# A transformer pair on one core: units and silu of the last block in another order

## The chip, the cores and the metric

The kernel runs on one core of a Trainium2 chip. The metric is the device time of one execution in microseconds (us). Below, PE is TensorE's matmul, DVE is VectorE, ACT is ScalarE, POOL is GpSimd and SP issues the loads of the weights.

## What is computed

Two blocks over 512 tokens of width 1024, in float32. The first is a mixer of banded attention and pooling with a convolutional feed-forward layer. The second, which matters here, adds to x the result of a mixer with four heads in two branches:

```python
hn = rms_norm_2(x, w_norm)
proj = jnp.einsum("bsd,de->bse", hn, w_in.astype(f32))
q_a, k_a, v_a, z_a, b_a, a_a, q_b, k_b, v_b, z_b = jnp.split(proj, idx, axis=-1)
qkv = jax.nn.silu(causal_depthwise_conv(jnp.concatenate([q_a, k_a, v_a], -1), conv_w))
beta = jnp.transpose(jax.nn.sigmoid(b_a), (0, 2, 1))
g = -jnp.exp(a_log) * jax.nn.softplus(a_a + dt_bias)
o_a = gated_delta_rule_chunked(q_a, k_a, v_a, g, beta)
o_a = rms_norm_2(o_a, gdn_norm_w) * jax.nn.silu(z_a)
o_b = diff_attention(q_b, k_b, v_b, lam)          # q_b, k_b normed and rotated
o_b = rms_norm_2(o_b, subln_w, SUBLN_EPS) * (1.0 - lam_init)
o_b = o_b * jax.nn.silu(z_b)
return jnp.einsum("bse,ed->bsd", jnp.concatenate([o_a, o_b], -1), w_out)
```

## The kernel before

Activations lie transposed, features on the 128 partitions and the 512 tokens along the free axis. Every product with weights is made in **units** of 128 x 1024 weights: eight steps (one for each tile of 128 input features), each of three matmuls of 512 columns, because weights and activations are split in a high and a low part (Wh and Wl, Hh and Hl; L514, L515, L517). SP loads a unit into `raw`, one of four buffers; ACT rounds it to Wh (L1697, `round_unit`); DVE takes the rest as Wl (L1029, `split`). Both do that two units ahead of the unit that PE works on. Behind its unit, DVE reads the sum out of its bank times the norm's factors (L1068).

The last block starts at about 703 us. DVE and ACT make the norm's tiles Hl and Hh; PE multiplies the first two units (c0 and c1 of the first head) along with them (`units_together`, L549), and adds up the squares (L568). The factors are a power on GpSimd (L2097), turned into a row by PE (`norm_row`, L585) and copied to RB by DVE (L1063). Without RB no unit can be read.

Then `second_block` runs four **stages**, one for each head a. Stage a has the prep of head a (decays, key products, the inverse of a triangular matrix in six levels) and, from the second stage on, the scan and the differential attention of head b = a - 1. A head has eight units: c0, c1, c2 (convolution inputs of q, k, v), z0 and z1 (gates of the two branches), Kr, Qb, v (second branch). Stage a computes c2 (first head only), z0, z1, Kr, Qb and v of head a, and c0, c1, c2 of the next head.

The order of the instructions is written out by `Rounds`: in each round every chain (prep, pair norms, scan, diff) goes one piece further, and then as many unit steps are issued as the pace says (PACE_PREP, PACE_SCORES). Each engine's program is made by the same rounds, so in a round PE, DVE and ACT have their parts of the same chains and of the same units. Engines are in order: a piece that waits holds up all that stands behind it. A unit's read and the rounding and splitting two units ahead are unit steps and fall where the count puts them.

The names that the prediction uses:
- `gate_chain`: PE multiplies the gates' rows (24 matmuls, L733 to L735), DVE copies them (L1323), PE turns them (into bank 5), DVE and ACT make beta and the logarithms `glog` (L1352), PE sums them (L751), DVE copies `gcum` (L1357).
- prep: the row of gcum (L759) into bank b6, DT (L1366), `sums` of squares (L826), kk (L769), LT (L1392) and its strips (L1394, L1395, ACT L1926), masks up to LmT (L1408); per level y (PE L778, ACT copy L1933) and t (PE L797, DVE L1422 and L1425, called T); level five has t at L801 and L804; kt and qk behind level two, then Kb (L1450), Kd, AT.
- pair norms: `pair sums` (PE L878), DVE L1471, a power on GpSimd (L2175), DVE L1476. The weighted copy of Kr and Qb and its square are ACT L2032 and L2033.
- scan of head b: for each of four tiles a product (L893), VN on DVE (L1485), products with Kd and QG (L898, L900), state St (L1492).
- diff of head b: maxima (L1544), exponentials (ACT L2000), Wd (L1563), turned (L952), product (L959). `out_norm` scales Oa or Od (L1509), PE turns it (L764), and DVE multiplies with Zs (L1514).
- `silu_gates(i)`: ACT makes Zs = silu(Zr) of head i once z0 and z1 are read (L1889). It is the first piece of the prep of stage i + 1, and for the last head it stands ahead of the tail.
- the convolution: ACT takes the first tap of C (L2023), DVE three more (L1579); c2's read first takes what is left of c1's taps.

In the tail the scan and diff of the last head run beside the output projection (L999, L1000, L1002), whose activations Hh are made from O by ACT (L2054).

Of the kernel before, what the change touches and what calls it, by code (L numbers as in the profile page):

```python
# [18 lines left out]
P = 128  # L19
# [7 lines left out]
GH = 4  # L27
# [54 lines left out]
PACE_SCALARS, PACE_END = 3, 1.5  # L82
PACE_SCORES, PACE_PREP = (None, 1.9, 1.9, 1.25), (1.5, 1.7, 1.7, 0.8)
# [66 lines left out]
def program(nc, ctx, x_in, w_units, w_ba, cols_in, mats_in, rope_in, rows_in, relb_in, counts_in,  # L150
# [144 lines left out]
    bank_of.update({G_UP + j: UP_BANKS[j % 6] for j in range(N_UP)})  # L295

# [4 lines left out]
    def sum_read(g):  # L301

        return bank_read[g % 2], g // 2 + 1
# [158 lines left out]

    UNIT_PLACE = {n: j for j, n in enumerate(("c0", "c1", "c2", "z0", "z1", "Kr", "Qb", "v"))}

# [17 lines left out]
    def second_block(rounds_of, first, chains_of, unit_of):  # L482

        for a, b in STAGES:
            st = rounds_of(a, b)
            st.scanning = st.scoring = b is not None
            st.dense = [unit_of(st, a, n) for n in ("c2", "z0", "z1", "Kr", "Qb", "v")[a > 0:]]
            if a + 1 < GH:
                st.dense += [unit_of(st, a + 1, n) for n in ("c0", "c1", "c2")]
# [13 lines left out]
    def tensor_program():  # L503
# [38 lines left out]
        def units_together(n0, g0, lags, turn, squares=None):  # L542


            banks = [group_begins(g0 + u) for u in range(len(lags))]

# [3 lines left out]
            for m in range(KT + max(lags)):  # L550
                now = [(u, m - lag) for u, lag in enumerate(lags) if 0 <= m - lag < KT]
                if m < KT:
                    pe.wait_ge(*norm_hh.at(turn, m))
                for u, k in now:
                    weights_ready(n0 + u, k)
                    product(u, k, Wh, Hh, start=k == 0, stop=False)
                    product(u, k, Wl, Hh, start=False, stop=False)
                if m < KT:
                    pe.wait_ge(*norm_dv.at(turn, ("hl", m)))
                for u, k in now:  # L560
# [168 lines left out]
        def gate_chain(st):  # L729
            pe.wait_ge(*lam_dv.at(0, "ba_lo"))  # L730
            for k in range(KT):
                w = slice(2 * GH * k, 2 * GH * (k + 1))
                pe.matmul(PS[0:2 * GH, 4, :], ba_h[:, w], Hh[:, k, :], start=k == 0, stop=False)  # L733
                pe.matmul(PS[0:2 * GH, 4, :], ba_h[:, w], Hl[:, k, :], start=False, stop=False)
                ins = pe.matmul(PS[0:2 * GH, 4, :], ba_l[:, w], Hh[:, k, :], start=False,  # L735
                                stop=k == KT - 1)
            ins.then_inc(*gate_pe.tick(0, "rows"))
            yield
            yield
# [174 lines left out]
        def diff(st, i):  # L914
# [11 lines left out]
            pe.wait_ge(*sum_read(G_P2 + 8 * i + UNIT_PLACE["v"]))  # L926
# [44 lines left out]
        def unit_of(st, a, name):  # L971
            j = UNIT_PLACE[name]
            n, g = U_P2 + 8 * a + j, G_P2 + 8 * a + j
# [3 lines left out]
        norm_row(2)  # L977
# [42 lines left out]
    def vector_program():  # L1020
# [564 lines left out]
        def read_of(st, a, name):  # L1585
            g = G_P2 + 8 * a + UNIT_PLACE[name]
# [28 lines left out]
        def unit_of(st, a, name):  # L1615
            n = U_P2 + 8 * a + UNIT_PLACE[name]
# [71 lines left out]
    def scalar_program():  # L1688
# [193 lines left out]
        def silu_gates(i):  # L1882

            ac.wait_ge(*sum_read(G_P2 + 8 * i + UNIT_PLACE["z0"]))
            ac.wait_ge(*sum_read(G_P2 + 8 * i + UNIT_PLACE["z1"]))
# [5 lines left out]
        def prep(st, i):  # L1891
# [20 lines left out]
            if i:  # L1912
                silu_gates(i - 1)
# [100 lines left out]
        def read_of(st, a, name):  # L2014
            g = G_P2 + 8 * a + UNIT_PLACE[name]
# [20 lines left out]
        def unit_of(st, a, name):  # L2036
            n = U_P2 + 8 * a + UNIT_PLACE[name]
# [216 lines left out]
def _layout(np, inp):  # L2254
# [16 lines left out]
    p2 = _units(np, big).reshape(8, GH, P, KT, P)[[0, 1, 2, 3, 7, 5, 4, 6]]  # L2271
    p2 = p2.transpose(1, 0, 2, 3, 4).reshape(32, P, KT, P)
# [72 lines left out]
```

## Time and profile before

| | us |
|---|---|
| median of 3 runs | 1111.91 |
| lowest and highest | 1110.41, 1115.26 |
| the profiled execution | 1109.57 |
| its span | 1108.1 |
| PE busy | 1062.4 (96%) |
| DVE busy | 646.0 (58%) |
| ACT busy | 443.2 (40%) |
| mean granted clock of PE | 0.989 |

Times of single instructions come from the one profiled execution. In a row of the timeline the bracket at the end is how long the engine sat idle before the instruction, and what ended that. In the chain of waits each piece is what the next one waited for; "issue" is time for which the profile has no record.

### The profile page before, as it was taken

The page shows a single profiled execution, that of the slowest core. Times are in us where ns is not written, and L with a number is a line of the kernel's source. Part 1 is how long each engine was busy: PE and PEld are TensorE (multiplying, and loading weights), DVE is VectorE, ACT ScalarE, POOL GpSimd, SP SyncE. Part 2 cuts the span into 40 slices and gives each one's busy share as a digit, 9 for nine tenths or more (in the row PEclk, how much of TensorE's full clock was granted, in tenths as well). Part 3 has the DMA queues.
Part 4 walks back from the last instruction along what each step waited for, and adds up shares of the span by engine and source line. Part 5 has one row for each costly group of instructions (what it writes and reads, how often), then busy time and mean ns, then how long its engine had stood idle before and what let it go on. Part 6 is the DMA issues. An engine that isn't in the chain of part 4 may idle for free.

```text
span 1108.1 us, 15316 instructions
## 1 busy us (share of the span) xinstructions
PE 1062.4 (96%) x6212; PEld 842.2 (76%) x6212; DVE 646.0 (58%) x1121; ACT 443.2 (40%) x773; POOL 89.5 (8%) x77
## 2 busy tenths in 40 slices
PE   7999999999999999999999999989989989988998
PEld 6777777778788888888888888867766866866776
DVE  6645454556437788777772122655576566466574
ACT  6233232344443544444442222443264254354531
POOL 1000000000210000000001000001120120120210
PEclk9999999999999999999999999999999989989999
DMA  8221313122321333333322233131111111110102
GB/s 333 84 83 57 95 58 95 58 77 78 112 95 57 96 114 97 113 96 95 95 95 88 103 114 114 36 95 58 58 39 54 62 39 39 59 56 21 58 20 76
DMA packets 25429, 90.72 MB, mean 82 GB/s; under 512 B 2880, under 2 KB 3136, under 8 KB 25232
## 3 DMA queue, kind: packets, MB, share of 16 engines
q1 hardware_dynamic: 23328, 83.90, 24.0%
q0 software_dynamic: 592, 3.54, 0.8%
q10 hardware_dynamic: 1440, 2.31, 0.6%
q8 instruction: 49, 0.80, 0.3%
q14 instruction: 20, 0.16, 0.0%
HBM read 87.64 MB, written 2.10 MB: 81 GB/s over the span
## 4 chain that ended last, share of the span: by engine, by line
PE 88%; DVE 7%; ACT 3%; issue 2%; POOL 0%; DMA 0%; ACTq 0%; DVEq 0%; POOLq 0%
PE PS L514 23%; PE PS L517 22%; PE PS L515 22%; PE PS L549 5%; PE PS L640 1%; DVE Wl L1029 1%; PE PS L769 1%; PE PS L1002 1%; PE PS L999 1%; PE PS L1000 1%; PE PS L653 1%; PE PS L946 1%; DVE C L1579 1%; ACT Wh L1697 1%; PE PS L663 1%
## 5 line engine op out<-in xcount | busy, mean ns | idle before, releaser
L514 PE MATMUL PS<-Hh,Wh 128*128 128x512 f32 x856 | 353.0, 412 | 0.6 <-ACT M L1817 0.6
L517 PE MATMUL PS<-Hh,Wl 128*128 128x512 f32 x856 | 336.1, 393 | 0.0
L515 PE MATMUL PS<-Hl,Wh 128*128 128x512 f32 x856 | 336.0, 392 | 0.0
L1029 DVE TENSOR_TENSOR Wl<-raw,Wh 128x1024 fp32r<-128x1024 f32 x155 | 188.9, 1224 | 193.9 <-ACT Wh L1697 192.1
L514 PEld LDWEIGHTS PS<-Hh,Wh 128*128 128x128 f32 x856 | 162.2, 189 | 44.4 <-issue 11.5
L1697 ACT ACTIVATE Wh<-raw 128x1024 fp32r<-128x1024 f32 x155 | 161.4, 1051 | 71.8 <-PE PS L517 60.9
L517 PEld LDWEIGHTS PS<-Hh,Wl 128*128 128x128 f32 x856 | 161.9, 189 | 35.2
L515 PEld LDWEIGHTS PS<-Hl,Wh 128*128 128x128 f32 x856 | 162.7, 190 | 31.6 <-issue 2.2
L514 PE MATMUL PS<-Ah,Wh 128*128 128x512 f32 x176 | 69.8, 396 | 0.0
L515 PE MATMUL PS<-Al,Wh 128*128 128x512 f32 x176 | 69.8, 396 | 0.0
L517 PE MATMUL PS<-Ah,Wl 128*128 128x512 f32 x176 | 69.8, 396 | 0.0
L1816 ACT ACTIVATE sq<-PS 128x512 f32<-128x512 f32 x16 | 9.6, 598 | 88.8 <-PE PS L517 88.8
L1068 DVE TENSOR_TENSOR tmp<-PS,RB 128x512 f32<-128x512 f32 x44 | 30.3, 692 | 21.0 <-PE PS L517 18.8
L1844 ACT ACTIVATE conv<-conv 128x512 f32<-128x512 f32 x22 | 13.9, 632 | 71.0 <-DVE conv L1271 71.0
L2107 POOL MEMSET ssum<- 128x512 f32 x2 | 1.1, 528 | 481.5 <-DVE Hl L1256 255.6
L517 PEld LDWEIGHTS PS<-Ah,Wl 128*128 128x128 f32 x176 | 33.1, 188 | 8.1
L515 PEld LDWEIGHTS PS<-Al,Wh 128*128 128x128 f32 x176 | 33.1, 188 | 8.1
L514 PEld LDWEIGHTS PS<-Ah,Wh 128*128 128x128 f32 x176 | 33.1, 188 | 8.1
L549 PE MATMUL PS<-Hh,Wh 128*128 128x512 f32 x72 | 30.1, 419 | 7.6 <-DVE Wl L1134 7.3
L1831 ACT ACTIVATE conv<-tmp,cols 128x512 f32<-128x512 f32 x44 | 35.2, 802 | 5.5 <-DVE tmp L1068 5.5
L1768 ACT ACTIVATE sq<-sq,nmax 128x512 f32<-128x512 f32 (+3 forms) x32 | 17.7, 554 | 44.3 <-DVE nmax L1194 43.7
L1271 DVE SCALAR_TENSOR_TENSOR conv<-tmp,cols,conv 128x510 f32<-128x510 f32 x44 | 33.0, 750 | 1.6
(310 smaller groups left out, 1479.0 us busy)
## 6 DMA issues: line engine op xcount, KB each, us to landing
raw<-in_w_units SPq DMA_DIRECT2D x155, 512.0 KB, 3.5
relb<-in_rel POOLq DMA_DIRECT2D x1, 2048.0 KB, 9.4
out<-X ACTq DMA_DIRECT2D x8, 256.0 KB, 2.1
X<-in_x SPq DMA_DIRECT2D x3, 512.0 KB, 7.4
X<-in_x SPq DMA_DIRECT2D x2, 256.0 KB, 4.3
raw<-in_w_units SPq DMA_DIRECT2D x2, 256.0 KB, 4.6
rope<-in_rope POOLq DMA_DIRECT2D x1, 512.0 KB, 4.0
mats<-in_mats POOLq DMA_DIRECT2D x1, 384.0 KB, 3.4
```

What stands on the lines that cost most here:

```text
L514: pe.matmul(bank, Wh[:, s, w], rhs[0](r), start=first and j == 0, stop=False)
L515: pe.matmul(bank, Wh[:, s, w], rhs[1](r), start=False, stop=False)
L517: ins = pe.matmul(bank, Wl[:, s, w], rhs[0](r), start=False, stop=last and end)
L549: return pe.matmul(banks[u], w[:, s, own], h[:, k, :], **ends)
L640: pe.matmul(PS[:, 2 + a, 0:nk], Q2[r, tok(qt)], K2[r, 0:nk], start=True, stop=True).then_inc(*att_pe.tick(i, ("scores", n, a)))
L1029: dv.tensor_tensor(Wl[:, s, :], raw[:, s, :], Wh[:, s, :].bitcast(F32), sub).then_inc(unit_split, 1)
L1068: return dv.tensor_tensor(dst, PS[:, bank_of[g], :], RB[:], mult).then_inc(bank_read[g % 2], 1)
L1271: dv.scalar_tensor_tensor(out=c[:, 2:], in0=y[:, 0:S - 2], scalar=col(C_CONV + 4 * j), in1=c[:, 2:], op0=mult, op1=add).then_inc(up_taps, 1)
L1697: ac.activation(Wh[:, s, :], raw[:, s, :], ACT.Copy).then_inc(unit_rounded, 1)
L1768: ac.activation(w, w, ACT.Exp, bias=nmax[:, b + a:b + a + 1], scale=1.0, accum_out=rsum[:, b + a:b + a + 1]).then_inc(*att_ac.tick(i, ("ex ...
L1831: ac.activation(conv[:, p % 2, j % 2, :], tmp[:, j % 2, :], ACT.Identity, bias=col(C_CONV + 4 * j + 3), scale=col(C_CONV + 4 * j + 2)).the ...
L1844: ac.activation(c, c, ACT.Gelu_apprx_tanh).then_inc(up_gelu, 1)
```

## The change

It touches the last block alone. The units are put in an order of their own by stage (`STAGE_UNITS`, `UNIT_PLACE`): z1 of a head moves to the start of the next head's stage (for the last head it is the last unit of its own), v comes ahead of Kr, z0 behind Qb. The paces change. The matmuls of the gates' rows move out of `gate_chain` in between the norm's tiles, and `norm_row` moves into `gate_chain`, behind four steps of the third unit (c2), for which that unit gets bank 6. `silu_gates` of the head before moves behind the silu of C, and that of the last head into the tail's fourth round. The weights are laid out in the new order.

```diff
+STAGE_UNITS = [[(a, x) for x in ("c2", "z0", "v", "Kr", "Qb")] if a == 0 else
+               [(a - 1, "z1"), *((a, x) for x in ("v", "Kr", "Qb", "z0", *("z1",) * (a == GH - 1)))]
+               for a in range(GH)]
+for a in range(GH - 1):
+    STAGE_UNITS[a] += [(a + 1, x) for x in ("c0", "c1", "c2")]
+UNIT_PLACE = {u: n for n, u in enumerate([(0, "c0"), (0, "c1"), *sum(STAGE_UNITS, [])])}
...
-PACE_SCALARS, PACE_END = 3, 1.5
-PACE_SCORES, PACE_PREP = (None, 1.9, 1.9, 1.25), (1.5, 1.7, 1.7, 0.8)
+PACE_GATES, PACE_END = (4, 2, 3, 3, 4, 5, 2, 1), 1.5
+PACE_SCORES, PACE_PREP = (None, 1.9, 1.9, 1.5), (1.3, 1.9, 1.9, 1.3)
...
+    bank_of[G_P2 + 2] = 6
...
-                while st.chains:
-                    st(PACE_SCALARS)
+                for pace in PACE_GATES:
+                    st(pace)
...
+                if turn == 2 and m < KT:
+                    w = slice(2 * GH * m, 2 * GH * (m + 1))
+                    pe.matmul(PS[0:2 * GH, 4, :], ba_h[:, w], Hh[:, m, :], start=m == 0, stop=False)
+                    pe.matmul(PS[0:2 * GH, 4, :], ba_l[:, w], Hh[:, m, :], start=False, stop=False)
                 if m < KT:
                     pe.wait_ge(*norm_dv.at(turn, ("hl", m)))
+                if turn == 2 and m < KT:
+                    ins = pe.matmul(PS[0:2 * GH, 4, :], ba_h[:, w], Hl[:, m, :], start=False,
+                                    stop=m == KT - 1)
...
         def gate_chain(st):
-            pe.wait_ge(*lam_dv.at(0, "ba_lo"))
-            for k in range(KT):
...
-            ins.then_inc(*gate_pe.tick(0, "rows"))
-            yield
+            yield
+            norm_row(2)
             yield
             pe.wait_ge(*gate_dv.at(0, "rows"))
...
+            else:
+                pe.wait_ge(*sum_read(G_P2 + 2))
             row_of(b6, gcum[:, i, :]).then_inc(*prep_pe.tick(i, "g"))
...
         units_together(U_P2, G_P2, LAGS_LAST, 2, up_squares)
-        norm_row(2)
...
                 ac.activation(C3[:], C3[:], ACT.Silu).then_inc(*prep_ac.tick(i, "silu"))
+                if i:
+                    silu_gates(i - 1)
                 yield
...
             if i:
-                silu_gates(i - 1)
                 yield from idle(2)
...
+        def last_gates():
+            yield from idle(3)
+            silu_gates(GH - 1)
+
         st = Rounds()
-        silu_gates(GH - 1)
-        st.chains = [split_outputs(st), scan(st, GH - 1), diff(st, GH - 1)]
+        st.chains = [split_outputs(st), scan(st, GH - 1), diff(st, GH - 1), last_gates()]
```

## Rows read from the trace of the kernel before

**Rows 1.** The page, part 1: busy us, share of the span, instructions.

```profile
PE 1062.4 (96%) x6212; PEld 842.2 (76%) x6212; DVE 646.0 (58%) x1121; ACT 443.2 (40%) x773; POOL 89.5 (8%) x77
```

**Rows 2.** Windows: length, busy time by engine, PE's clock, DMA share, GB/s.

```profile
800.00:885.00 85.00, 78.57 (x704) 61.30 (x704) 52.80 (x116) 37.09 (x79) 14.66 (x10) 0.98 0.17 52
885.00:970.00 85.00, 78.57 (x690) 61.10 (x687) 51.86 (x116) 37.08 (x79) 14.44 (x10) 0.96 0.16 50
970.00:1042.00 72.00, 63.36 (x617) 48.62 (x614) 43.55 (x106) 35.06 (x76) 13.49 (x10) 0.93 0.14 44
```

**Rows 3.** Timeline of PE: start, us, what, and idle before it with its releaser.

```profile
723.47 0.65 PE L585 MATMUL PS<-ident,rstd 128*128 128x128 f32 x4 [1.34 <-POOL rstd L2097]
743.42 0.37 PE L751 MATMUL PS<-glog,mats 128*128 128x16 f32 x2 [2.26 <-DVE glog L1352]
764.47 0.45 PE L778 MATMUL PS<-head_Ti,head_LmT 32*32 32x32 f32 x32 [1.69 <-DVE head_LmT L1408]
809.54 0.49 PE L898 MATMUL PS<-head_VN,head_Kd 128*128 128x128 f32 x2 [3.94 <-DVE head_VN L1485]
845.79 1.16 PE L769 MATMUL PS<-C 128*128 128x128 f32 x8 [2.09 <-DVE head_Ti L1425]
893.53 0.79 PE L898 MATMUL PS<-head_VN,head_Kd 128*128 128x128 f32 x2 [3.94 <-DVE head_VN L1485]
978.84 0.80 PE L898 MATMUL PS<-head_VN,head_Kd 128*128 128x128 f32 x2 [4.64 <-DVE head_VN L1485]
1013.47 0.44 PE L952 MATMUL PS<-ident,head_Wd 128*128 128x128 f32 x2 [1.31 <-DVE head_Wd L1563]
```

**Rows 4.** The chain that ended last, 884 to 895: start, us, what.

```profile
884.37 0.76 DVE C L1579
...
886.69 0.61 DVE Yc L1068
...
888.07 1.28 ACT L1889
...
889.36 1.06 ACT Zs L1889
890.42 0.95 ACT Wh L1697
...
891.43 1.10 issue
```

**Rows 5.** A window behind the third stage's start.

```profile
892.00:900.00 8.00, 6.47 (x17) 4.72 (x18) 6.38 (x11) 4.38 (x5) 4.03 (x3) 0.57 0.22 66
```

**Rows 6.** Timelines of PE and DVE at the entry, 723 to 731.

```profile
723.88 0.48 PE L733 MATMUL PS<-Hh,ba_h 128*8 128x512 f32 x1
729.51 0.39 PE L514 MATMUL PS<-Hh,Wh 128*128 128x512 f32 x1
...
724.16 0.69 DVE L1063 COPY RB<-PS 128x512 f32<-128x512 f32 x1 [1.83 <-PE PS L585]
...
730.40 0.67 DVE L1323 COPY tmp<-PS 8x512 f32<-8x512 f32 x1
```

**Rows 7.** Timelines of ACT and DVE in the first head, 758 to 765.

```profile
758.07 0.72 ACT L2032 ACTIVATE heads_Kr<-Yc,cols 128x512 f32<-128x512 f32 x1 [4.60 <-DVE Yc L1068]
...
760.29 1.23 DVE L1029 TENSOR_TENSOR Wl<-raw,Wh 128x1024 fp32r<-128x1024 f32 x1 [0.98 <-ACT Wh L1697]
761.43 0.68 DVE L1392 TENSOR_TENSOR head_LT<-PS,head_DT 128x512 f32<-128x512 f32 x1
...
763.77 0.65 DVE L1408 TENSOR_TENSOR head_LmT<-head_Ti,mats 128x512 f32<-128x512 f32 x1
```

**Rows 8.** Timelines of DVE and POOL in the first head, 773 to 779.

```profile
773.19 0.69 DVE L1450 TENSOR_TENSOR head_Lo<-PS,eg 128x512 f32<-128x512 f32 x1 [0.66 <-PE PS L764]
...
775.59 2.90 POOL L2175 TENSOR_TENSOR rqk_b<-rqk_b,half 128x16 f32<-128x16 f32 x1 [0.18 <-DVE rqk_b L1471]
```

**Rows 9.** Timeline of DVE in the second stage, at the sums.

```profile
823.02 0.17 DVE L1377 TENSOR_SCALAR rqk<-PS 128x8 f32<-128x8 f32 x1 [1.12 <-PE PS L826]
```

More of the change, by code:

```diff
@@ L460, in program @@
     N16 = GH * NT
-    UNIT_PLACE = {n: j for j, n in enumerate(("c0", "c1", "c2", "z0", "z1", "Kr", "Qb", "v"))}
     def unit_steps(st, name, unit):
@@ L486, in second_block @@
             st.scanning = st.scoring = b is not None
-            st.dense = [unit_of(st, a, n) for n in ("c2", "z0", "z1", "Kr", "Qb", "v")[a > 0:]]
-            if a + 1 < GH:
-                st.dense += [unit_of(st, a + 1, n) for n in ("c0", "c1", "c2")]
+            st.dense = [unit_of(st, *u) for u in STAGE_UNITS[a]]
             if b is None:
                 st.chains.append(first(st))
-                while st.chains:
-                    st(PACE_SCALARS)
+                for pace in PACE_GATES:
+                    st(pace)
+                assert not st.chains
             st.chains = chains_of(st, a, b)
@@ L545, in units_together @@
             banks = [group_begins(g0 + u) for u in range(len(lags))]
+            if turn == 2:
+                pe.wait_ge(*lam_dv.at(0, "ba_lo"))
             def product(u, k, w, h, **ends):
@@ L557, in units_together @@
                     product(u, k, Wl, Hh, start=False, stop=False)
+                if turn == 2 and m < KT:
+                    w = slice(2 * GH * m, 2 * GH * (m + 1))
+                    pe.matmul(PS[0:2 * GH, 4, :], ba_h[:, w], Hh[:, m, :], start=m == 0, stop=False)
+                    pe.matmul(PS[0:2 * GH, 4, :], ba_l[:, w], Hh[:, m, :], start=False, stop=False)
                 if m < KT:
                     pe.wait_ge(*norm_dv.at(turn, ("hl", m)))
+                if turn == 2 and m < KT:
+                    ins = pe.matmul(PS[0:2 * GH, 4, :], ba_h[:, w], Hl[:, m, :], start=False,
+                                    stop=m == KT - 1)
+                    if m == KT - 1:
+                        ins.then_inc(*gate_pe.tick(0, "rows"))
                 for u, k in now:
@@ L729, in gate_chain @@
         def gate_chain(st):
-            pe.wait_ge(*lam_dv.at(0, "ba_lo"))
-            for k in range(KT):
[L732 to L736, printed above, removed]
-            ins.then_inc(*gate_pe.tick(0, "rows"))
             yield
+            norm_row(2)
             yield
@@ L925, in diff @@
             pe.matmul(s1, mat(K_SWAP), Qs[:, i % 2, :], start=True, stop=True).then_inc(*diff_pe.tick(i, "qs"))
-            pe.wait_ge(*sum_read(G_P2 + 8 * i + UNIT_PLACE["v"]))
+            pe.wait_ge(*sum_read(G_P2 + UNIT_PLACE[i, "v"]))
             if i:
@@ L971, in unit_of @@
         def unit_of(st, a, name):
[L972 to L973 removed]
+            n, g = U_P2 + UNIT_PLACE[a, name], G_P2 + UNIT_PLACE[a, name]
             yield from unit_steps(st, name, unit(n, g))
         units_together(U_P2, G_P2, LAGS_LAST, 2, up_squares)
[L977 removed]
         second_block(lambda a, b: Rounds(), gate_chain, chains_of, unit_of)
@@ L1585, in read_of @@
         def read_of(st, a, name):
-            g = G_P2 + 8 * a + UNIT_PLACE[name]
+            g = G_P2 + UNIT_PLACE[a, name]
             def conv_read():
@@ L1615, in unit_of @@
         def unit_of(st, a, name):
-            n = U_P2 + 8 * a + UNIT_PLACE[name]
+            n = U_P2 + UNIT_PLACE[a, name]
             yield from unit_steps(st, name, unit(n, read_of(st, a, name)))
@@ L1882, in silu_gates @@
         def silu_gates(i):
-            ac.wait_ge(*sum_read(G_P2 + 8 * i + UNIT_PLACE["z0"]))
-            ac.wait_ge(*sum_read(G_P2 + 8 * i + UNIT_PLACE["z1"]))
+            ac.wait_ge(*sum_read(G_P2 + UNIT_PLACE[i, "z0"]))
+            ac.wait_ge(*sum_read(G_P2 + UNIT_PLACE[i, "z1"]))
             if i:
@@ L2014, in read_of @@
         def read_of(st, a, name):
-            g = G_P2 + 8 * a + UNIT_PLACE[name]
+            g = G_P2 + UNIT_PLACE[a, name]
             def first_tap_of():
@@ L2036, in unit_of @@
         def unit_of(st, a, name):
-            n = U_P2 + 8 * a + UNIT_PLACE[name]
+            n = U_P2 + UNIT_PLACE[a, name]
             yield from unit_steps(st, name, unit(n, read_of(st, a, name)))
@@ L2269, in _layout @@
     big = np.concatenate([w2[:, :n], w2[:, n + 2 * GH:]], axis=1)
-    p2 = _units(np, big).reshape(8, GH, P, KT, P)[[0, 1, 2, 3, 7, 5, 4, 6]]
-    p2 = p2.transpose(1, 0, 2, 3, 4).reshape(32, P, KT, P)
+    p2 = _units(np, big).reshape(8, GH, P, KT, P)
+    part = {n: j for j, n in enumerate(("c0", "c1", "c2", "z0", "Qb", "Kr", "v", "z1"))}
+    p2 = np.stack([p2[part[x], a] for a, x in sorted(UNIT_PLACE, key=UNIT_PLACE.get)])
     wout = _units(np, inp["w_out_2"][0])
```

## The prediction

> **What bounds the kernel now.** The page comes first. TensorE (PE) is busy 96% of the span [rows 1], so the time is PE's work plus what PE waits plus what it loses to a lower clock. Everything the diff touches lies in the last block, from about 703 us to the end, and each of those three has to be read there. The windows by head give idle and clock: PE idles 6.4 us of 85 in the second head's stage, and 8.6 of 72 in the fourth's at a mean clock of 0.93 [rows 2]. The timeline of PE, kept to instructions that waited, then names the waits [rows 3]: at the entry 1.34 us for the norm's factors and 2.26 for the gates' logarithms; 1.69 in the first head for the masks of the inverse (LmT); 3.94, 3.94 and 4.64 at the start of the three later stages, each time on VN, the scan's first vector step; and 2.09 in the middle of the second and third heads. In the fourth stage the window's idle is 8.64, of which 4.64 is the start; the other 4.0 are five waits of 0.4 to 1.3, the 1.31 among them.
>
> **What a start is made of.** The chain of waits over the third stage's start is to be read downwards [rows 4]: DVE drains three taps of C (0.76 each) and reads the unit, ACT takes the first tap, loads a table (1.28), computes Zs (1.06), and only then rounds the next unit (0.95); DVE splits it (1.10), and VN is queued behind that split. So the silu of the gates stands in the path of a vector step with which it has nothing to do.
>
> **A unit of cover.** A unit has eight steps of three matmuls. The 24 gate-row matmuls run from 723.88 to 729.51 [rows 6], 0.23 each, so a step is 0.69 us. I counted, from the rounds and paces, which steps stand between two chain instructions on PE, and what DVE and ACT have queued between theirs. The order so counted for the kernel before agrees with its timelines; for the changed one it gives the terms below.
>
> **1. Entry.** The 24 gate-row matmuls move in between the norm's tiles. PE is the slower engine there too, so they only change place: 5.6 us less behind the factors' row, 5.6 more ahead: nothing. The first four steps of the third unit go ahead of the factors' row, 2.75 us, and cover the 1.34 wait. But between that row and the turning of the gates' rows PE now has two steps left, where it had 24 matmuls and six steps. DVE's part between the two is unchanged: from the copy of RB at 724.16 to that of the rows, which ends at 731.07, and PE's row began 0.7 earlier, together 7.6 us [rows 6, 3]. PE's cover is 0.4 + 1.4. A new wait of 5.8 us. Behind it, eleven steps (third unit's rest excepted) now stand where eight did, so the 2.26 for the logarithms goes. Entry: 5.8 - 1.34 - 2.26 = +2.2. Bounds: +1.5 if the later copy is met a step sooner, +3 if the slower clock behind the wait delays the next read.
>
> **2. First head, the inverse's start.** In the new order the read of Kr stands behind LT, and the split of two units ahead behind that read, ahead of the masks. From the end of kk: LT, strips and masks 3.0 (LT starts at 761.43, LmT ends at 764.42), and in between them a read, 0.7, weighted copy and square on ACT, 1.3 (from 758.07 to a rounding's length before the split), the rounding 1.0 and the split 1.1 (760.29 to 761.43): with small hand-overs 7.0 [rows 4, 7]. PE has one step, four transposes and three steps, 3.2. With 0.2 by which DVE is late for sums: wait 4.0, for 1.69: +2.3. Bounds +1 and +3.
>
> **3. First head, the pair sums.** Qb's read now stands behind Kb, Kd and AT on DVE, and PE's pair sums three rounds further on have two steps of cover. From Kb at 773.19 DVE is taken until the pair factors start on GpSimd at 775.59, 2.2 without the hand-over [rows 8]; then read, weighted copy and square, 2.0. A new wait of 2.2; bounds 0 and 2.5.
>
> **4. First head, levels four to six.** The pair factors take GpSimd 2.90 [rows 8] and T4 is queued behind them; c0's read, its first tap and a rounding stand ahead of Y5 on ACT (0.7 + 0.7 + 1.0 for 2.5 of cover), and a split and two taps ahead of T5 on DVE. Waits of 0.4, 2.0 and 1.0: +3.4; bounds 0 and 4.
>
> **5. Starts of the later stages.** Silu's load and Zs leave the path: 2.34 [rows 4]. At the second stage two of the three taps are already taken in the prep rounds (1.5 more), so 3.94 falls to about 0.2. At the third and fourth a split now sits ahead of the last reads of the head before and hands 0.4 back: 3.94 to 2.0, and 4.64 to 2.1, since the pace of 1.5 puts one more step ahead of the wait. Together 12.5 to 4.3: -8.2. Zs goes behind C's silu, where ACT needs no second load; the rounding there waits for z1's read and Zs and comes 1.7 later. Queued behind it on DVE are the scan's second state and the first maximum; behind those DVE idled 1.12 for the sums [rows 9], which hides it but for half a microsecond that PE's own cover there takes. Without that cover it costs 1.7 a head. The mid-head waits of 2.09 have the same queues ahead of them as before: nothing.
>
> The 1.28 of the load ends where Zs starts, 888.07 to 889.36 [rows 4]. The Trainium skill, "ScalarE: Activation LUTs", section "What ACT_TABLE_LOAD costs", puts a drain of about 1.38 us behind every load. The trace doesn't show it here. By the page each start would give 1.4 more, and the time would be some 3 us less than my sum.
>
> **6. Fourth stage.** One unit more (z1 of the head before) fills it, at 1.5 steps a round for 1.25. But the splits fall elsewhere: one ahead of the fourth VN (0.8), and Kr's read, weighted copy, rounding and split now all stand ahead of the scaling of Oa (1.0 + 1.1 + 1.3 + 0.7 against three steps: 2.1); then 0.9 for Wd, 0.2, and 1.4 for Y5 behind Qb's copy. 5.5 for 4.0: +1.5. Bounds -3 and +3.
>
> **7. Clock.** Behind each of the three starts the granted clock fell from 2.4 to 1.2 GHz for a while, as 892 to 900 shows (0.57), and once behind the small waits at 1013 to 1020 [rows 2, 5]. By the three windows that is 85 x 0.02 + 85 x 0.04 + 72 x 0.07 = 10.1, of which some 0.6 fell into waits: 9.5 us. Waits of 2.26 and 2.09 drew no fall. Changed: the two waits of 4 us and more in the first head draw one each, 2.5 (between 1.7, that of 800 to 885, and 3.4, that of 885 to 970); the fourth stage keeps its 1.7; 0.7 for the levels' waits. 7.4: -2.1.
>
> **8. Tail.** The last silu goes three rounds back on ACT, behind the splitting of the outputs. No row shows it there; Zs and its load take 2.3, and ACT is the least busy of the three engines [rows 2]: nothing; bounds -0.5 and +1.
>
> **Sum.** 2.2 + 2.3 + 2.2 + 3.4 - 8.2 + 1.5 - 2.1 = +1.3 us on the profiled execution, whose span is 1108.1 and whose time is 1109.6. That is 2.3 below the median, 1111.9, from which the forecast is therefore 1113.2.
>
> **Rivals.**
> A, faster. The new waits are chains over three engines, and I let each link begin where the one before ends. If DVE and ACT reach them earlier than that, half of 4.0 + 2.2 + 3.4 + 5.5 = 15.1 goes, and one fall of the clock with it: 7.5 + 2.5 less, 1103. For it: DVE is busy 53 and ACT 37 of the 85 us of a stage [rows 2], and the starts' gain is read straight off a chain. Against: each is at most a few instructions long and queued in order. Chance 0.25.
> B, slower: the clock. The kernel before had one fall behind small waits. If the waits of 2 us (pair sums, levels, two starts) draw three falls more at 2.5, and the two long ones 3.4 instead of 2.5, it is 7.5 + 1.8 more, 1122.5; with the long ones alone it is 1115, with one short fall 1117.5, and from the second on the kernel is slower. For it: the fourth stage. Against: 2.26 and 2.09 twice without. Chance 0.2.
> C, the change doesn't do what it says: the silu still holds up the units, now by z1's read. If DVE's idle isn't there, three heads lose 1.7 each: 1118.3. Chance 0.08.
> The forecast: 0.47, with its own range of 1108 to 1118 from the bounds of terms 2, 4 and 6.
>
> **How the numbers follow.** The forecast is the likeliest, 1113.2. Leaving the far halves of A and B out, the range is 1104 to 1121. About 0.5%, 5.6 us, is what a measurement tells from no change: faster than 1106.3 are most of A and a little of the forecast, 0.26; slower than 1117.5 most of B, half of C and a little of the forecast, 0.27; between, 0.47.
>
> **What the profile after would show.** Step 1: an idle of about 5.8 before the transposes of the gates' rows into bank 5, none before those of the factors or the sums of glog. 2: about 4 before the first matmuls of the inverse. 3, 4: 2 before the pair sums, 2 before the level-five products. 5: under 2.5 before each first Kd product, and half as many table loads per later head. 6: 2 before the turning of Oa in the last stage. 7: granted clock under 1 behind steps 1 and 2 and none from 890 to 900. The prediction is wrong if 5.8 isn't there, or if first-head idle sums to less than 8.

## The result, and the profile after

The changed kernel takes 1117.84 us (median of 4 runs, 1117.39 to 1119.57) for 1111.41 beside it (4 runs): ratio 1.0054, 95% interval 1.0038 to 1.0069. The medians differ by 6.4 us, the ratio (of means) gives 6.0. That is slower, just past the 0.5% that the prediction called the edge of what can be told from no change, inside its range, and 4.6 above its forecast of 1113.2. The profiled execution has a span of 1116.4 us, 8.3 more than that of before.

The page, part 1, for [rows 1]:

```profile
PE 1068.4 (96%) x6212; PEld 844.9 (76%) x6212; DVE 646.5 (58%) x1121; ACT 435.0 (39%) x767; POOL 89.7 (8%) x77
```

The same instructions, less six table loads on ACT (773 to 767, 443.2 to 435.0 us). PE does the same number of matmuls in 6 us more: a lower clock. The windows, for [rows 2] (the first is the entry and the first head):

```profile
700.00:800.00 100.00, 86.65 (x681) 67.26 (x680) 54.05 (x100) 37.96 (x60) 8.47 (x9) 0.90 0.15 48
800.00:885.00 85.00, 81.20 (x721) 63.57 (x722) 53.33 (x117) 35.40 (x79) 13.69 (x10) 0.98 0.17 56
885.00:970.00 85.00, 80.92 (x699) 63.15 (x698) 52.07 (x115) 34.52 (x77) 13.97 (x11) 0.96 0.16 51
970.00:1042.00 72.00, 64.35 (x622) 48.69 (x621) 45.02 (x106) 31.82 (x74) 12.13 (x10) 0.98 0.15 45
```

And of before, the first window, which the prediction had not looked at:

```profile
700.00:800.00 100.00, 93.93 (x767) 74.08 (x767) 59.92 (x109) 41.56 (x65) 8.39 (x9) 1.00 0.18 57
```

So the later stages gained: PE is busy 81 of 85 us where it was 78.6. The first 100 us lost: PE idles 13.3 for 6.1, and its clock is 0.90 for 1.00. PE's timeline names the waits, for [rows 3]; start, us, what, and the idle before it:

```profile
738.98 0.59 PE L753 MATMUL PS<-ident,tmp 8*128 8x8 f32 x4 [5.60 <-DVE tmp L1334]
770.03 0.65 PE L789 MATMUL PS<-head_Ti,head_LmT 32*32 32x32 f32 x32 [3.72 <-DVE head_LmT L1419]
783.74 1.95 PE L891 MATMUL PS<-mats,sq 128*128 128x2 f32 x16 [1.93 <-ACT sq L2045]
797.04 0.22 PE L812 MATMUL PS<-head_Ti 32*32 32x32 f32 x2 [1.46 <-ACT head_Ti L1945]
800.37 0.67 PE L797 MATMUL PS<-T,head_LT 64*64 64x64 f32 x8 [0.62 <-DVE T L1448]
816.77 0.49 PE L911 MATMUL PS<-head_VN,head_Kd 128*128 128x128 f32 x2 [0.79 <-DVE head_VN L1496]
899.01 0.49 PE L911 MATMUL PS<-head_VN,head_Kd 128*128 128x128 f32 x2 [1.57 <-DVE head_VN L1496]
982.95 0.49 PE L911 MATMUL PS<-head_VN,head_Kd 128*128 128x128 f32 x2 [1.90 <-DVE head_VN L1496]
1025.06 0.66 PE L775 MATMUL PS<-ident,head_Oa 128*128 128x128 f32 x4 [1.58 <-DVE head_Oa L1520]
```

The three long waits at the starts (3.94, 3.94, 4.64) have become 0.79, 1.57 and 1.90; 5.60, 3.72 and 1.93 are new or longer, in the first 100 us. All of PE's waits from 700 us on sum to 31.9 us, for 30.7.

**The clock** was read in windows of 1 us over the whole span. It falls for one of two lengths: from 2.4 to 1.2 GHz for 3.4 us, which loses 1.7 us, or for 6.8, which loses 3.4 ("double" below). From 700 us on, before had four falls, two of them double: 10.2 us lost (and one more at 326, ahead of the last block). After has eight, two double: 700, 738 (double), 769 (double), 786, 878, 912, 936 and 984: 17.1 us lost. Three windows of after, laid round a fall each:

```profile
738.00:746.00 8.00, 7.02 (x21) 5.63 (x22) 4.89 (x8) 2.79 (x3) 0.00 (x0) 0.57 0.21 66
769.00:777.00 8.00, 6.97 (x109) 5.03 (x110) 2.14 (x6) 0.29 (x2) 0.00 (x0) 0.57 0.22 68
877.00:883.00 6.00, 6.00 (x30) 5.41 (x28) 4.09 (x7) 2.27 (x3) 0.42 (x1) 0.72 0.07 14
```

8 us at 0.57 is 3.4 us lost, 6 us at 0.72 is 1.7. The first two begin in the last microsecond of the waits of 5.60 and 3.72, at 738.3 and 769.0, and reach into the work behind them. In the third PE is busy for all 6 us, and it had no wait over 0.3 since 852. So the profiled executions differ from 700 us on by 1.2 us of waits and 6.8 of clock, 8.0 of 8.3; 1.7 of the 6.8 are the fall at 700, which lies ahead of the change. Two questions were left: which edit makes what, and whether the waits draw the falls or these come by chance.

### The profile page after: what moved, and what is told of

Its sections match the earlier page's. It is cut to its first block, busy times and chain, and to the rows that moved or that the text cites. A ratio compares the mean times of both kernels' runs of the same rounds, so it can differ in the third digit from the quotient of the medians.

```text
span 1116.4 us, 15311 instructions
## 1 busy us (share of the span) xinstructions
PE 1068.4 (96%) x6212; PEld 844.9 (76%) x6212; DVE 646.5 (58%) x1121; ACT 435.0 (39%) x767; POOL 89.7 (8%) x77
## 4 chain that ended last, share of the span: by engine, by line
PE 85%; DVE 8%; ACT 3%; issue 2%; POOL 1%; DMA 1%; SPq 0%; ACTq 0%; DVEq 0%; POOLq 0%
PE PS L521 22%; PE PS L524 21%; PE PS L522 21%; PE PS L558 4%; DVE Wl L1040 2%; ACT Wh L1708 1%; PE PS L658 1%; PE PS L780 1%; PE PS L1013 1%; PE PS L1010 1%; PE PS L1011 1%; PE PS L671 1%; DVE C L1590 1%; PE PS L959 1%; DVE Yc L1079 1%
## 5 line engine op out<-in xcount | busy, mean ns | idle before, releaser
L558 PE MATMUL PS<-Hh,Wh 128*128 128x512 f32 x72 | 30.2, 420 | 7.8 <-DVE Wl L1145 7.0
L2035 ACT ACTIVATE C<-Yc,cols 128x512 f32<-128x512 f32 x12 | 8.6, 721 | 66.1 <-DVE Yc L1079 66.1
```

Of the source, the lines that this page charges most:

```text
L558: return pe.matmul(banks[u], w[:, s, own], h[:, k, :], **ends)
```

## The experiments

All kernels compute everything. Ratios are against runs of the kernel before on the same chip. "Waits" is the sum of PE's idle from 700 us on, "clock" what the falls from 700 us on lost, both in the profiled execution. "Clock, runs" is the mean over a kernel's runs of span times (1 - granted clock); it takes in the fall near 326, and for after a fifth run. The granted clock of a run is on record to 0.001, which is 1.1 us, so these means are good to some tenths.

| kernel | median us (runs) | ratio, 95% interval | waits | clock | clock, runs |
|---|---|---|---|---|---|
| before | 1112.3 (65) | 1 | 30.7, 30.2 | 10.2, 11.9 | 15.1 |
| after | 1117.84 (4) | 1.0054 (1.0038 to 1.0069) | 31.9, 32.2 | 17.1, 17.1 | 17.4 |
| b_silu | 1107.10 (6) | 0.9956 (0.9938 to 0.9974) | 27.9 | 11.9 | 10.1 |
| b_entry | 1115.33 (4) | 1.0038 (1.0023 to 1.0053) | 31.5 | 17.1 | 17.8 |
| b_third | 1108.54 (10) | 0.9972 (0.9962 to 0.9983) | 28.1 | 13.7 | 14.7 |
| a_old_entry | 1114.12 (6) | 1.0023 (1.0010 to 1.0035) | 29.8 | 13.7 | 14.8 |
| a_p15 | 1113.03 (10) | 1.0001 (0.9986 to 1.0015) | 27.6 | 17.1 | 15.8 |
| b_silu_third | 1107.96 (11) | 0.9948 (0.9928 to 0.9967) | 25.3 | 11.9 | 12.0 |
| a_third_p15 | 1104.15 (6) | 0.9927 (0.9907 to 0.9947) | 23.9 | 11.9 | 11.2 |
| a_awake | 1115.16 (10) | 1.0034 (1.0017 to 1.0050) | 20.8 | 11.9 | 8.6 |
| best_awake | 1102.20 (6) | 0.9906 (0.9887 to 0.9925) | 15.0 | 6.8 | 7.7 |
| best_awake2 | 1100.93 (5) | 0.9893 (0.9874 to 0.9911) | 14.3 | 1.7 | 6.2 |

Two figures stand where a kernel was profiled twice. The run that was profiled is not always a typical one: it was the slowest of its kernel for b_silu, b_entry, a_p15 and a_awake, and the fastest for best_awake2.

### The silu alone

**b_silu**: the kernel before with `silu_gates` in its new place (and that of the last head in the tail's fourth round, which the cut below leaves out), nothing else.

```diff
                 ac.activation(C3[:], C3[:], ACT.Silu).then_inc(*prep_ac.tick(i, "silu"))
+                if i:
+                    silu_gates(i - 1)
                 yield
...
             if i:
-                silu_gates(i - 1)
                 yield from idle(2)
```

> The kernel before with the silu's new place alone (behind C's silu, and in the tail's fourth round). My theory: the load and Zs, 2.34 us, leave the path of each of the three starts, so their waits of 3.94, 3.94 and 4.64 go to about 1.6, 1.6 and 2.3 (7.0 us less), and the two long and the one short fall of the clock behind them (3.0 + 3.0 + 1.7 us) go too: 1096 to 1099. Rival, falls come nearly as often behind short waits: one or two short ones of 1.7 stay, 1099 to 1102. Rival, the silu still holds up the units because the rounding now waits for it in the sixth round: less than 3 us gained, 1108 or more.

Measured: 1107.1 us, 4.9 faster where 13 to 16 were expected. The starts fell as said (3.94 to 1.57 twice, 4.64 to 2.28), but a new wait came up nine us behind the first two of them. ACT's, DVE's and PE's timelines of b_silu around it:

```profile
819.02 1.04 ACT L1889 ACTIVATE Zs<-Zr 128x1024 f32<-128x1024 f32 x1
...
820.16 0.69 DVE L1068 TENSOR_TENSOR Zr<-PS,RB 128x512 f32<-128x512 f32 x1 [3.39 <-ACT Zs L1889]
820.77 0.28 DVE L1485 TENSOR_TENSOR head_VN<-head_U,PS 128x128 f32<-128x128 f32 x1
...
821.10 0.80 PE L898 MATMUL PS<-head_VN,head_Kd 128*128 128x128 f32 x2 [2.32 <-DVE head_VN L1485]
```

Read upwards: PE waits for the second VN; VN stands on DVE behind the read of z0 of the next head; and that read waits 3.39 us because it writes Zr, which Zs still reads. In the old order of the units the next z0 is the first unit of a stage, so a later silu collides with it. In the changed kernel z0 stands behind Qb, the unit in that place is z1 of the head before, and Zs waits for it anyway. Its DVE and ACT at the same place:

```profile
822.36 0.69 DVE L1079 TENSOR_TENSOR Zr<-PS,RB 128x512 f32<-128x512 f32 x1 [0.69 <-PE PS L524]
822.97 0.28 DVE L1496 TENSOR_TENSOR head_VN<-head_U,PS 128x128 f32<-128x128 f32 x1
...
821.24 1.28 ACT L1915 ACT_TABLE_LOAD   x1
822.54 1.49 ACT L1915 ACTIVATE C<-C 128x1536 f32<-128x1536 f32 x1
823.93 1.04 ACT L1900 ACTIVATE Zs<-Zr 128x1024 f32<-128x1024 f32 x1
```

So this edit and the new order of the units belong together: the change's own waits show none at the second scan step of the second and third stage.

### The entry alone, and its two halves

**b_entry**: the kernel before with the entry of after. **a_old_entry**: after with the entry of before. **b_third**: the kernel before with four steps of the third unit ahead of the factors' row, but the gates' rows left behind it (the paces of the first eight rounds, 4, 3, 3, 3, 4, 4, 2, 1, are not in the cut below):

```diff
+            yield
+            norm_row(2)
             pe.wait_ge(*lam_dv.at(0, "ba_lo"))
             for k in range(KT):
...
-        norm_row(2)
```

> The kernel before with the new entry alone: gates' rows in between the norm's tiles, third unit in bank 6 with four steps ahead of the factors' row, and the new paces of the eight first rounds. My theory: a wait of 5.6 ahead of the turning of the gates' rows for the 1.34 and 2.26 that go, +2.0, and a long fall of the clock behind it, +3: 1116 to 1117. Rival, the clock falls without regard to that wait: 1113 to 1114. Rival, the entry is what the change gains by: under 1110.

> The changed kernel with the entry of before (gates' rows behind the factors' row, that row right behind the two first units, eight rounds of three steps). My theory: the wait of 5.6 and the long fall behind it go, 1.34 and about 2.2 for the logarithms come back: 5 us less than the changed kernel, 1112 to 1114, and the waits in the first head (3.7, 1.9, 1.5, 0.6) stay as they are. Rival, those waits come from the entry too: 1108 or less.

> The kernel before with four steps of the third unit (in bank 6) ahead of the factors' row, but with the gates' rows left behind that row, where they and three more steps cover the copy on VectorE. My theory: neither the 1.34 nor the 5.6 is there, and eleven steps ahead of the logarithms' sums cover the 2.26: 3.6 us less than before, 1107 to 1109. Rival, the gates' rows are covered but the steps are missing later on in the first head, whose rounds had none to spare: the same as before, 1110 to 1112.

Measured: the entry alone makes the kernel before 0.38% slower, and taken out of after it leaves 1114.1 of 1117.8, with the first head's waits as they were (3.69, 1.93, 1.52). The two halves of the entry go opposite ways. PE's timeline of b_entry, then of b_third:

```profile
739.43 0.59 PE L748 MATMUL PS<-ident,tmp 8*128 8x8 f32 x4 [5.60 <-DVE tmp L1330]
```

```profile
742.64 0.37 PE L754 MATMUL PS<-glog,mats 128*128 128x16 f32 x2 [1.00 <-DVE glog L1356]
```

With the gates' rows behind the factors' row there is no wait at the turn; 1.34 goes, 2.26 becomes 1.00, and the kernel is 0.28% faster. The third unit ahead of the row is worth having; moving the rows is what makes the 5.60.

### The first head's pace

**a_p15**: after with one number put back.

```diff
-PACE_SCORES, PACE_PREP = (None, 1.9, 1.9, 1.5), (1.3, 1.9, 1.9, 1.3)
+PACE_SCORES, PACE_PREP = (None, 1.9, 1.9, 1.5), (1.5, 1.9, 1.9, 1.3)
```

> The changed kernel with one number put back: the first head's pace 1.5 steps a round for 1.3, the new entry as it is. If the pace makes the first head's waits, 3.72 falls to 1.7, 1.93 goes, the levels' 2.1 to 0.8, and the second stage's start goes from 0.8 to 2.2, because the steps are used up earlier: the waits from 700 us sum to 28 for 31.9. With the double stretch at 1.2 GHz behind 3.72 now a single one (1.7 less) and the one behind 1.93 gone (1.7 less) the time is about 1110.5. Rival: the new order of the units makes them (Kr's and Qb's reads behind LT and Kb), not the pace; then they stay within 0.5 us and the time is 1116 to 1119.

Measured: 1113.0 us, level with before, waits 27.6. With the new order of the units and the old pace the three waits of the first head are gone or as before. What the pace of 1.3 does in the old order was not run.

```profile
770.85 0.45 PE L789 MATMUL PS<-head_Ti,head_LmT 32*32 32x32 f32 x32 [1.69 <-DVE head_LmT L1419]
...
789.60 0.45 PE L808 MATMUL PS<-head_Ti 32*32 32x32 f32 x32 [0.40 <-ACT head_Ti L1945]
792.69 0.44 PE L794 MATMUL PS<-head_Ti,head_LT 32*32 32x32 f32 x16 [0.37 <-DVE head_Ti L1436]
805.84 0.49 PE L906 MATMUL PS<-St,head_Wt 128*128 128x128 f32 x2 [2.16 <-ACT head_U L1967]
```

3.72 is 1.69 again, 1.93 is gone, the levels lost most of theirs. The 2.16 is the price: the stage has used its steps up, and the first scan has no cover. The waits fell as the first theory said (27.6 for 28), the time by 4.8 where it said 7.3: the double fall behind LmT became single, but the clock as a whole lost as much as in after in the profiled execution, the slowest of ten. In the mean of the runs it lost 15.8 for 17.4.

### The parts that gain, together

**b_silu_third** puts the silu's new place and b_third together. **a_third_p15** is after with the gates' rows back behind the factors' row and the pace 1.5.

> The kernel before with the silu's new place and with four steps of the third unit ahead of the factors' row (the gates' rows left behind it). The two edits touch waits that lie 80 us apart, so I expect their gains to add: PE's waits from 700 us on sum to 30.67 before, 27.88 with the silu alone, 28.05 with the entry alone, so 25.3 together. Ratio about 0.9956 x 0.9972 = 0.993, some 1104 us. Rival, the clock: what is saved in waits is given back as stretches at 1.2 GHz at other places, because the granted clock does not depend on PE's waits; then the waits still sum to 25.3 but the lost clock is above the 12 to 14 us of the two single runs, and the time is 1106 to 1109.

> The changed kernel with the gates' rows back behind the factors' row (the third unit's four steps stay ahead of it) and with the first head's pace at 1.5 steps a round, as before, in place of 1.3. My account of the change: the wait of 5.60 at the gates' turn is there only because the rows moved ahead of the factors' row, so it goes, and with it the 1.34; about 1.0 stays at the logarithms. The waits of 3.72 and 1.93 in the first head come from the lower pace and fall to about 2.0 and 0. The starts stay at 0.8, 1.6 and 1.9. Waits from 700 us sum to 23 to 25 for 31.9, and the time is 1105 to 1109. Rival: the first head has one unit fewer than before in its stage, so a pace of 1.5 uses its steps up early and the last levels of the inverse have no cover: waits of 2 us and more appear from 797 to 812, the sum stays above 27, and the time is 1111 or more.

Measured: b_silu_third has exactly the waits that were expected, 25.3, but its time is 1108.0 where 1104 was expected, no better than the silu alone. The waits and the time are those of the rival, but the lost clock is not: 11.9 us, not above 12 to 14. The eleven runs fall in two groups, five at 1102.1 to 1103.9 us with a granted clock of 0.992 or 0.993, six at 1108.0 to 1110.0 with 0.986 or 0.987; the profiled one is of the second. So the gain is there in some executions and lost to the clock in others. a_third_p15 is faster than before by 0.73% and than after by 1.3%. So units, silu and the third unit together are a gain; the rows' place (a_p15 against a_third_p15, 1.0001 and 0.9927) and the pace of 1.3 (after against a_p15, 1.0054 and 1.0001) turned it into a loss. What the new order with the later stages' paces adds by itself is not shown: a_third_p15 has it and b_silu_third has not, 0.9927 for 0.9948, and their intervals overlap. Its rival was right in part: the 2.16 at the first scan is there too, but the sum is low all the same.

### The same kernels once more

> The kernel before, word for word, once more. If PE's waits decide where the granted clock falls, the falls come at the same places as in the first profile: 326, 810, 892, 978 and 1022 us, two of them double (3.4 us lost each), 12 us in all. If they come by chance, their places and number move between two executions of one program by as much as they do between two kernels, and the waits stay the same to 0.1 us.

> The changed kernel, word for word, once more. In its first profile eight falls of the granted clock from 700 us on lost about 17 us: at 700, 738 and 769 (double), 786, 878, 912, 936 and 984. If they follow the waits, 738, 769 and 786 come again, right behind the waits of 5.60, 3.72 and 1.93, and so may 984 behind the 1.90; those at 878 and 912, which no wait of PE is near, tell most: if they move or are gone, part of the 6.9 us by which the clock differs from the kernel before is a matter of the execution; if they are there again, the program's order makes them in a way that PE's waits do not show.

Measured: 1111.35 and 1118.1 us. The waits are the same to 0.1 us, but for a few near a fall that differ by 0.3 to 0.5. The falls are not the same. In the second execution of before there are seven, all single: the double ones at 892 and 978 are single, and 767, 849 and 934 are new. The same stretch, 10 us behind the third start, in the first execution and in the second:

```profile
891.00:901.00 10.00, 7.47 (x23) 5.55 (x23) 6.99 (x11) 6.36 (x8) 4.03 (x3) 0.66 0.17 52
```

```profile
891.00:901.00 10.00, 6.07 (x24) 4.33 (x23) 6.61 (x10) 6.37 (x7) 2.48 (x3) 0.83 0.18 52
```

And PE's waits of 2.09 and 2.10, behind which the first execution had none:

```profile
848.07 1.19 PE L769 MATMUL PS<-C 128*128 128x128 f32 x8 [2.09 <-DVE head_Ti L1425]
...
933.43 1.22 PE L769 MATMUL PS<-C 128*128 128x128 f32 x8 [2.10 <-DVE head_Ti L1425]
```

Here PE's clock falls about 1 us behind each. After falls at seven of its eight places again, 878 and 912 among them, and at 963 in place of 984. So a fall behind a wait of about 2 us is a matter of the execution (of 2.26, 1.69, 2.09 and 2.10, none in the first one of before and three in the second), but a fall behind a long one is not. From 700 us on the eleven profiles of the kernels without filling hold 19 waits of 3.69 us and more, and none between 2.4 and 3.6. Each of the 19 has a fall at its end: 18 begin 0.4 to 1.9 us before PE has work again, one 1.4 us behind, and 12 are double. A double one can stand at a shorter wait too: that of b_silu at 820.8, where PE's wait of 2.32 ends at 821.10.

### Work in place of waits

**a_awake**: after, with matmuls whose results nobody reads ahead of its three large waits.

```diff
+            fill_wait(20, 5)
             pe.wait_ge(*gate_dv.at(0, "rows"))
...
+                if i == 0 and lv == 1:
+                    fill_wait(13, B_SCAN)
...
+            if i == 0:
+                fill_wait(6, B_S[0])
             pe.wait_ge(*qk_ac.at(i, "Qb"))
```

> The changed kernel with PE kept at work in three waits: 20, 13 and 6 matmuls of 128x256 (0.23 to 0.25 us each at full clock, whose results nobody reads) ahead of the waits of 5.60, 3.72 and 1.93. PE's own work of the kernel and the end of each wait stay where they are, so the remaining idle there is 0.6 to 1.0 each and no instruction starts later. Theory one, an idle PE draws the stretches at 1.2 GHz behind these waits: those at 738 (3.4 us lost), 769 (3.4) and 786 (1.7) go, the granted clock lost from 700 us on is about 8.5 for 17.1, and the time is 1109 to 1111. Theory two, the stretches have nothing to do with the waits: 1117 to 1119 with the same three, or more if the fillers at 1.2 GHz run past the end of the wait. Between: the stretches become single ones, 1114.

Measured: 1115.2 us, 2.7 faster than after, although the filling was too long. By time alone the two can't be told apart (1.0017 to 1.0050, and 1.0038 to 1.0069); the clock tells them apart. PE's timeline of a_awake at the three places:

```profile
733.34 8.79 PE L786 MATMUL PS<-cols,ident 128*128 128x256 f32 x40
...
766.89 5.77 PE L786 MATMUL PS<-cols,ident 128*128 128x256 f32 x26
...
781.71 2.75 PE L786 MATMUL PS<-cols,ident 128*128 128x256 f32 x12
```

I had taken a record in the profile for one matmul, but 20 of these are recorded as 40: each takes 0.44 us, not 0.23. So the three fillings ran 8.8 - 5.6, 5.8 - 3.7 and 2.75 - 1.9, together 6.1 us, past the ends of the waits. The clock in three windows laid over the fillings and what follows them:

```profile
733.00:747.00 14.00, 14.00 (x67) 11.80 (x66) 9.04 (x14) 4.44 (x6) 0.00 (x0) 1.00 0.13 39
766.00:774.00 8.00, 8.00 (x80) 6.42 (x81) 3.20 (x6) 2.47 (x4) 0.00 (x0) 1.00 0.24 69
781.00:791.00 10.00, 10.00 (x143) 8.20 (x141) 3.35 (x7) 2.74 (x5) 2.50 (x2) 1.00 0.18 54
```

All three falls are gone, and none comes until 829. Falls at 829 and 853 are new, so this execution, the slowest of ten, still lost 11.9 us from 700 us on for 17.1. The mean loss over the runs drops from 17.4 to 8.6 us, 8.8, where the three falls had lost 8.5, and no run of a_awake (5.6 to 13.4 us lost) comes near one of after (16.7 to 20.1). So 6.1 us more work and 8.8 less of clock make the 2.7. That settles it for these three: PE's idle draws the falls, which theory two excluded. The filling also moves what follows by up to 6 us, but that is no rival: the 19 long waits lie at many different times, and each had its fall.

**best_awake** does the same in a_third_p15, in four waits (1.68, 2.16 and twice 2.10); **best_awake2** fits the fillings to the waits and adds two starts and the logarithms.

> The kernel with the third unit's steps alone at the entry and a first-head pace of 1.5 (1104.15 us, seven falls of the clock from 700 us on, 11.9 us lost), with fillers of 5, 6, 6 and 6 matmuls of 128x256 in the waits of 1.68 (LmT), 2.16 (the first scan) and twice 2.10 (mid-head). Where idle draws the falls, those at 763, 797, 838 and 923, right behind these waits, go, up to 6.8 us: 1098 to 1100, while the three with no wait near them (865, 899, 950) stay or move. If falls come at some rate whatever the waits are, as their number from 700 us on suggests (seven in each of four kernels with quite different waits), others come in their place: 1103 to 1106.

> The kernel of best_awake (1102.2 us) with the fillers cut to the length of the waits, and one more place. A 128x256 filler is recorded as two instructions and takes 0.46 us, not 0.25: six of them took 2.75 where the wait was 2.10 to 2.16, five 2.32 where it was 1.68. Now 3, 4, 4 and 4 there, which gives back 0.5 to 0.6 each, about 2.1 in all; 1 of them ahead of the 1.00 at the logarithms; and 3 (1.4 us) ahead of the two starts of 1.89 and 1.90, in a bank that is free there. Where an idle PE draws the falls, those behind the starts (895, 977) go too, 3.4 us, unless the leftover of 0.3 to 0.5 us is enough to draw them: 1097 to 1100. Rival: the falls that are left, four in the profile of best_awake, come whatever is done (they are not right behind a wait); then the time falls by the 2.1 alone, to 1100, and with the shorter fillers falls may even come back behind 763 or 797: 1102 to 1104.

Measured: 1102.2 and 1100.9 us, 1.1% under before and 1.6% under after. PE's timeline of best_awake2 at one of the mid-head waits, and its clock from the entry's end to the end of the kernel:

```profile
833.91 1.89 PE L783 MATMUL PS<-cols,ident 128*128 128x256 f32 x8
835.64 0.60 PE L773 MATMUL PS<-ident,C 128*128 128x128 f32 x4
836.60 1.16 PE L778 MATMUL PS<-C 128*128 128x128 f32 x8 [0.37 <-DVE head_Ti L1446]
```

```profile
742.00:1096.00 354.00, 336.49 (x2901) 262.33 (x2900) 220.17 (x481) 147.50 (x324) 57.36 (x40) 1.00 0.17 52
```

In the profiled execution (1097.5 us) no fall is left in 354 us; what is left is 14.3 us of waits, 9.7 of them in thirteen waits of the fourth stage and the tail. This is its best: the five runs lost 3.3 to 8.8 us to the clock. The intervals of a_third_p15, best_awake and best_awake2 touch or overlap (0.9907 to 0.9947, 0.9887 to 0.9925, 0.9874 to 0.9911), so how much each set of fillings is worth in time is not settled; the mean clock loss goes from 11.2 over 7.7 to 6.2 us. What speaks against "each fall stands right behind its own wait": a_third_p15 had falls at 865, 899 and 950, and after at 878 and 912, with no wait near. They come in step with waits further back: 26 to 28 us behind a mid-head wait (852 and 878 in after, 838 and 865 in a_third_p15, 923 and 950) and 12 or 13 behind a start (899 and 912, 887 and 899). In the profiled executions they are gone where these waits are filled: best_awake, with the mid-head waits filled, has only those behind two starts (883 and 895, 965 and 977) and one at 1021, and best_awake2, with these starts filled, none of them. But the one at 1021 is gone too, though the waits near it (1.23 and 1.59) were left, and the profile of best_awake2 is its lightest execution. So that the far falls hang on those waits is likely, not shown, and how a wait would act so far ahead, no run here shows.

## Why the prediction came out as it did

By its own steps, with the measured value behind the forecast one:

| step | forecast | measured | |
|---|---|---|---|
| 1 entry | 5.8 - 1.34 - 2.26 = +2.2 | 5.60 - 1.34 - 2.26 = +2.0 | right |
| 2 inverse's start | 4.0 for 1.69: +2.3 | 3.72: +2.0 | right |
| 3 pair sums | +2.2 | +1.9 | right |
| 4 levels | 0.4, 2.0, 1.0: +3.4 | none, 1.46, 0.62: +2.1 | too large |
| 5 starts | 12.5 to 4.3: -8.2 | 12.5 to 4.26: -8.3 | right in sum |
| 6 fourth stage | 5.5 for 4.0: +1.5 | 5.74: +1.7 | right |
| 7 clock | -2.1 | +6.8 (first pair), +5.1 (second) | wrong, in sign too |
| 8 tail | 0 | the same waits of 0.58, 0.30, 0.86, 0.73 and 0.93 | right |

**The waits** were forecast at +3.4 us and came to +1.5 by the table (+1.2 by the sums over all waits, +2.0 in the second pair). The working by order, rounds and durations comes within 0.3 us in steps 1, 2, 3 and 6 and in the sum of step 5. It was too large where three engines hand over in turn, in step 4: the 0.4 at level four isn't there, and the two others are 0.4 to 0.5 smaller. Rival A had said that chains over three engines would come out shorter, but its size (half of 15.1 us) was far off. A small part may be that an engine's next instruction begins before the modelled end of the last, by 0.1 us in ACT's rows above (822.54 + 1.49 for 823.93); link by link it was not followed.

Within step 5 the parts moved: the second stage's start is 0.79 for 0.2, the third's 1.57 for 2.0, the fourth's 1.90 for 2.1. Rival C, the silu holding up the units, is half there: the rounding behind it does wait, and DVE idles 2.7 us ahead of the split, but the cover of DVE's idle and PE's own queue held, so PE shows no wait. DVE's timeline of after:

```profile
825.95 1.22 DVE L1040 TENSOR_TENSOR Wl<-raw,Wh 128x1024 fp32r<-128x1024 f32 x1 [2.70 <-ACT Wh L1708]
```

Where the units are not reordered, in b_silu, C is a wait of 2.3 us twice.

**The table load.** In the trace of after the silu begins 0.02 us behind the end of the load (821.24 + 1.28 to 822.54, above). The Trainium skill, "ScalarE: Activation LUTs", section "What ACT_TABLE_LOAD costs", puts a drain of about 1.38 us behind the load; by it the starts, as the prediction worked out, would have gained some 3 us beyond the forecast 8.2, and they gained 8.3. The trace disagrees with the drain, and the measurement decides.

**The clock**, step 7, is the step that failed: forecast at -2.1 us, it measured +6.8 in the first pair of profiles and +5.1 in the second. Four premises were wrong. First, "waits of 2.26 and 2.09 drew no fall" was read off one execution; in another of the same kernel three of four such waits have one. Second, the long waits of the first head were priced at 2.5 each, between a single and a double fall, and are double in both executions: 3.4 each. Third, the falls at the starts were to leave and nothing to take their place; those right behind 816 and 899 did leave, but falls stand at 786, 878, 912, 936 and 984. The forecast allowed 7.4 us for the last block, measured are 15.4, and 1.7 more for a fall at 700 that lies ahead of the change. Fourth, the profile before was a light one: its falls lost 12.2 us over the span (1108.1 x 0.011), and the mean of 65 runs is 15.1. The 2.3 us between its time and the median fit that: runs of before at 1110 to 1111 us have a granted clock of 0.987 to 0.989, those at 1115 one of 0.983 to 0.985. The prediction added them as an offset of unknown kind, which was right for the sum, but read them as nothing that the clock term should heed. Counted over runs, the clock's part of the change is 17.4 - 15.1 = +2.3 for -2.1. With the +1.2 to +2.0 of waits that makes 3.5 to 4.3 of the 6.0 us of the ratio; the rest is not assigned.

**The rivals.** B had the mechanism: it gave 1122.5 for long falls at 3.4 each and three more short ones, 1117.5 for one more. The time is 1117.8, since the waits came out 1.4 to 2.2 us under the forecast, fewer falls were added than it allowed, and the baseline had more than I had read. B deserved more than 0.2, because the row that spoke for it (a fall behind waits of 1.3) and those that spoke against it (three waits without one) were of the same kind and of one execution. The signs that the prediction set are there: 5.60 ahead of the gates' turn, 3.72 ahead of the inverse, 1.93 and 1.46, all starts under 2.5, a granted clock under 1 behind steps 1 and 2. Only the last of them, none from 890 to 900, was a sign of the starts alone: it is there too, but the falls went to 878 and 912. The first head's idle in steps 2 to 4 is 7.7 us, under the 8 below which the prediction called itself wrong. That is step 4's doing, 2.1 for 3.4. That the time still lies only 4.6 us above the forecast is partly luck: the waits were put about 2 us too high, and the clock 4.4 too low by the runs (8.9 by the first pair of profiles).

## What to carry to other kernels

Where the engine that sets the time is nearly full, count the cover between each pair of dependent instructions after a reordering: taking 24 matmuls out from behind a row gave nothing where they went and a wait of 5.6 us where they had stood. Edits made together should be tried apart, since here three of them together gain 0.7% and two lose it again, and in the silu's case the waits that it saves are saved whole only along with the new order of the units. And before pricing a clock, profile the same kernel twice; where waits can't be removed, work of their length in their place is worth trying. The kernel before does so already ahead of the last block, with the matmuls of L591.

## What the runs showed of the hardware

The clock falls come in two lengths, 3.4 and 6.8 us at 1.2 GHz, 1.7 and 3.4 us lost; no other was seen in fourteen profiles, but for some that begin in the last microsecond of the kernel. All 19 waits of 3.69 us or more from 700 us on drew one. Waits of about 2 us drew one or not from one execution of the same program to another. With waits of 5.60, 3.72 and 1.93 filled with work, the falls behind them were gone, and with seven waits filled the last block had one left in its lightest execution, at its beginning. One execution's clock loss can be 3 us off the mean and more: 12.2 to 18.9 in 65 runs of the kernel before, whose mean is 15.1.

A matmul of 128x256 in float32 is recorded as two instructions and takes 0.44 us; 20 of them took 8.79.
